# A hybrid decoder step on one core: the first tile's front in another order, one weight place less, two row places more

## What is computed

```
mod = silu(c) @ w_ada + b_ada                       # six vectors per request
h = rmsnorm(x) * (1 + scale1) + shift1
q, k, v, u, gv, gate_a, gate_b = h @ w_in           # 7 x 1024 columns
out_b = stick_breaking_attention(q, k, v)           # 8 heads x 128, no softmax
out_a = u * (w_spatial @ layernorm(gelu(gv)) + b)   # 128 x 128 per channel group
x = x + gate1 * ((gate_a * (out_a @ w_ba) + gate_b * (out_b @ w_bb)) @ w_out)
h = rmsnorm(x) * (1 + scale2) + shift2
for each token and each of 8 heads:                 # retrieval
    scores against 2 x 128 sub-keys -> best 16 of 16 x 16 pairs -> 16 expert numbers
    coef = softmax(best) * gelu(h . down[expert]);  sum += coef * up[expert]
y = rmsnorm(x + gate2 * sum)
```

## Time and profile before

| | us |
|---|---|
| median of three timed runs (lowest, highest) | 2500.59 (2497.98, 2501.23) |
| the profiled execution | 2490.67 |
| its span, first to last instruction | 2488.5 |
| TensorE busy in it | 1888.3 (76%) |
| VectorE busy | 1558.6 (63%) |
| GpSimd busy | 1265.7 (51%) |
| ScalarE busy | 572.2 (23%) |

### The profile page before, as it was taken

How to read it: one execution, slowest core, us unless ns; L and a number is a source line. 1 busy time by engine, 2 the same in 40 slices (tenths; PEclk the granted TensorE clock), 3 DMA queues, 4 the chain that set the end, 5 groups by cost and what they waited for, 6 DMA issues and landing times.

```text
span 2488.5 us, 25049 instructions
## 1 busy us (share of the span) xinstructions
PE 1888.3 (76%) x7944; PEld 1316.6 (53%) x7944; DVE 1558.6 (63%) x3451; ACT 572.2 (23%) x1217; POOL 1265.7 (51%) x1169
## 2 busy tenths in 40 slices
PE   4876879777896767876878699877666577677777
PEld 2666868666775555644655466656454222222222
DVE  1011166789887467754587767675769987767662
ACT  1060121664110112134222310111011122122121
POOL 0000035556664454643556555555557777776763
PEclk7998989898998898987986765888888789999999
DMA  7867779988999797984799889999989999999996
GB/s 271 346 242 241 265 270 376 399 298 341 389 411 359 252 396 284 407 304 168 285 359 378 352 320 371 338 365 365 348 322 343 337 390 395 393 409 408 409 409 269
DMA packets 219219, 845.04 MB, mean 340 GB/s; under 512 B 26576, under 2 KB 35848, under 8 KB 197585
## 3 DMA queue, kind: packets, MB, share of 16 engines
q0 software_dynamic: 165888, 604.05, 63.7%
q1 hardware_dynamic: 36884, 216.87, 23.0%
q10 hardware_dynamic: 16316, 22.52, 2.6%
HBM read 826.29 MB, written 16.80 MB: 339 GB/s over the span
## 4 chain that ended last, share of the span: by engine, by line
PE 39%; DMA 20%; DVE 15%; POOL 8%; issue 8%; ACT 5%; DVEq 5%; SPq 1%; ACTq 1%; POOLq 0%
PE bank L822 12%; PE bank L1138 9%; PE bank L813 8%; DMA gather_ring<-in_expert_down,expert_numbers 8%; DMA gather_ring<-in_expert_up,expert_numbers 4%; DVE expert_sums L1831 4%; POOL gather_ring L778 3%; POOL gather_ring L763 3%; DVE gather_ring L1800 2%; DMA weight_chunks<-in_w_in 2%; DMA v_tokens<-in_expert_up,expert_numbers 1%; POOL weight_chunks L763 1%; DMA key_scores<-key_scores 1%; PE bank L1062 1%; SPq L671 1%
## 5 line engine op out<-in xcount | busy, mean ns | idle before, releaser
L763 POOL DMA_INDIRECT gather_ring<-in_expert_down,expert_numbers x488 | 569.3, 1167 | 797.7 <-DVEq L1763 357.9
L1138 PE MATMUL bank<-gather_ring,coef_diagonals 128*128 128x512 f32 x952 | 566.1, 740 | 327.9 <-ACT coef_diagonals L1416 191.1
L778 POOL DMA_INDIRECT gather_ring<-in_expert_up,expert_numbers x510 | 545.6, 1070 | 346.7 <-PE bank L1138 198.0
L1800 DVE CUSTOM_DVE_ANT_0 gather_ring<-gather_ring,h_tiles 128x1024 f32<-128x1024 f32 x408 | 498.3, 1226 | 234.8 <-DMA gather_ring<-in_expert_down,expert_numbers 213.2
L1138 PEld LDWEIGHTS bank<-gather_ring,coef_diagonals 128*128 128x128 f32 x952 | 204.9, 230 | 617.1 <-issue 370.5
L822 PE MATMUL bank<-hT,weight_chunks 128*128 128x128 f32 (+2 forms) x2304 | 408.3, 339 | 32.6 <-DMA weight_chunks<-in_w_in 19.5
L822 PEld LDWEIGHTS bank<-hT,weight_chunks 128*128 128x128 f32 x2304 | 380.5, 202 | 80.8 <-issue 59.6
L1831 DVE SCALAR_TENSOR_TENSOR expert_sums<-gather_ring,expert_coefs,expert_sums 128x1024 f32<-128x1024 f32 x269 | 345.5, 1285 | 9.4 <-issue 9.4
L813 PE MATMUL bank<-weight_chunks,hT 128*128 128x256 f32 x960 | 219.9, 389 | 20.7 <-DMA weight_chunks<-in_w_in 20.7
L813 PEld LDWEIGHTS bank<-weight_chunks,hT 128*128 128x128 f32 x960 | 185.8, 195 | 54.9 <-DMA weight_chunks<-in_w_in 24.2
L1416 ACT ACTIVATE coef_diagonals<-identity,expert_coefs 128x128 f32<-128x128 f32 x304 | 108.7, 393 | 285.1 <-DVE expert_coefs L1811 126.2
(11 more groups left out here) (242 smaller groups left out, 2109.7 us busy)
## 6 DMA issues: line engine op xcount, KB each, us to landing
weight_chunks<-in_w_in SPq DMA_DIRECT2D x84, 1024.0 KB
weight_chunks<-in_w_ada SPq DMA_DIRECT2D x24, 1024.0 KB
weight_chunks<-in_w_query SPq DMA_DIRECT2D x24, 1024.0 KB
weight_chunks<-in_w_branch_a SPq DMA_DIRECT2D x12, 1024.0 KB
weight_chunks<-in_w_branch_b SPq DMA_DIRECT2D x12, 1024.0 KB
weight_chunks<-in_w_out SPq DMA_DIRECT2D x12, 1024.0 KB
weight_chunks<-in_cache_k SPq DMA_DIRECT2D x16, 512.0 KB
weight_chunks<-in_cache_v SPq DMA_DIRECT2D x16, 512.0 KB
```

The lines of the kernel that those rows point to most:

```text
L763: pool.indirect_dma_start(out=d_row(slot), out_offset=None, in_=down, in_offset=bass.IndirectOffsetOnAxis(ap=expert[:, t, h * TOPK + k:h * ...
L778: pool.indirect_dma_start(out=u_row(slot), out_offset=None, in_=up, in_offset=bass.IndirectOffsetOnAxis(ap=expert[:, t, h * TOPK + k:h * T ...
L1138: mm = nc.tensor.matmul(bank[6 + half], diag[:, n % 8, :], u_row(slot)[:, half * 512:(half + 1) * 512], start=(u == PE_TILE[t][0]), stop=( ...
L1800: nc.vector.tensor_tensor_reduce(out=row, in0=row, in1=x, scale=1.0, scalar=0.0, op0=ALU.mult, op1=ALU.add, accum_out=dots[:, m % 2, k:k + ...
```

## The change

The two row buffers and the weight buffer change sizes: `NW` from 4 to 3, `D_EARLY` from 4 to 5, `U_EARLY` from 5 to 6; together they keep their size. Attention of tile 0 takes four heads at once, with instructions four times as wide, in four steps instead of six. The modulation vectors are stored behind the first three merge chunks, with six stores of the sampled vectors a quarter (one for each vector, repeated over the tokens of a sequence) for the eight of before. The norms of tiles 1 to 4 move into the front of group 0, beside its k chunks. The first head's scores are read where ScalarE leaves them, without the way through memory, and `exponentials(0)` and `weigh(0)` change places in their orders. The numbers `RAISE`, `WEIGH`, `AHEAD` and `LATER` are new names for values that stay as they were.

```diff
-D_EARLY, D_LATE = 4, 8
-U_EARLY, U_LATE = 5, 8
+D_EARLY, D_LATE = 5, 8
+U_EARLY, U_LATE = 6, 8
...
-    size = 2 if g == 0 else 1
+    size = 4 if g == 0 else 1
...
-NW = 4
+NW = 3
...
                 if g == 0:
+                    load_through("merge", g, NW - 1)
                     sp.wait_ge(s_modv, 4 * NMOD)
                     sp.wait_ge(s_mod, 8)
...
                         sp.dma_start(rows[:, :, q], modq[32 * q:32 * q + 1]).then_inc(s_modst, 16)
-                        for i in range(DSEQ):
-                            sp.dma_start(by_token[:, i, :, q], modq[32 * q + 1:32 * q + NG]).then_inc(s_modst, 16)
-                    sp.wait_ge(s_modst, 16 * 4 * (DSEQ + 1))
+                        for m in range(NMOD):
+                            sp.dma_start(by_token[:, :, m, q],
+                                         modq[32 * q + 1:32 * q + NG, m].unsqueeze(1).broadcast_to([NDEC, DSEQ, QUARTER])).then_inc(
+                                             s_modst, 16)
+                    sp.wait_ge(s_modst, 16 * 4 * (NMOD + 1))
...
+                def four_scores(b):
+                    z = bank[4 + b]
+                    nc.tensor.matmul(z[:, :].rearrange("p (j n) -> p j n", j=4), ident[:],
+                                     hidden[:].unsqueeze(1).broadcast_to([P, 4, P]), start=True, stop=False)
+                    for j in range(4):
+                        mm = nc.tensor.matmul(z[:, j * P:(j + 1) * P], kT[:, 0, 4 * b + j, :], q[:, 4 * b + j, 0:P],
+                                              start=False, stop=(j == 3))
+                    mm.then_inc(s_az, 4)
+
+                def four_exponents(b):
+                    pe.wait_ge(s_al, 4 * b + 4)
+                    if b:
+                        pe.wait_ge(s_aw, 4 * b)
+                    log, pos, neg = (att(what, 4 * b, g) for what in ("log", "pos", "neg"))
+                    nc.tensor.matmul(bank[2][:, :], since[:], log, start=True, stop=False)
+                    nc.tensor.matmul(bank[2][:, :], later[:], pos, start=False, stop=False)
+                    nc.tensor.matmul(bank[2][:, :], ident[:], neg, start=False, stop=True).then_inc(s_ac, 4)
...
+                def four_log_parts(b):
+                    log, pos, neg = (att(what, 4 * b, g) for what in ("log", "pos", "neg"))
+                    act.wait_ge(s_az, 4 * b + 4)
+                    for j in range(4):
+                        hd, cols = 4 * b + j, slice(j * P, (j + 1) * P)
+                        z = bank[4 + b][:, cols]
+                        nc.scalar.activation(log[:, cols], z, ACT.Abs, scale=SCALE, bias=bias_b[:, hd:hd + 1])
...
+                    nc.scalar.activation(log, log, ACT.Exp, scale=-1.0)
+                    act.drain()
+                    nc.scalar.activation(log, log, ACT.Ln, bias=1.0).then_inc(s_al, 4)
...
             for n, _ in enumerate(front(0)):
-                if n in (queries + 2, queries + 3):
-                    load_scores(act, n - queries - 2)
+                if n == queries + 3:
+                    load_scores(act, 1)
+                if n == queries + 5:
+                    exponentials(0)
+                    load_scores(act, 2)
             other = chain(front(1), front(2))
-            done = 0
-            exponentials(0)
-            load_scores(act, 2)
...
+            def first_norm(n):
+                x = vv[:, [t for ts in GROUPS for t in ts][n], :]
+                dve.drain()
+                mean_square(x, 0, s_n1v)
+                r = reciprocal_root(s_n1s, n + 1, 0)
+                nc.vector.tensor_scalar(x, x, r, None, ALU.mult).then_inc(s_n1h, 1)
...
                 for c in range(12):
                     if g == 0 and c % 4 == 3:
                         modulation(2 + c // 4)
+                    if g == 0 and 4 <= c < 8:
+                        dve.wait_ge(s_x[1 if c < 6 else 2], 32 * 2)
+                        first_norm(c - 3)
                     yield
...
-                dve.wait_ge(s_scld[c % 2], 16 * (c // 2 + 1))
+                if c:
+                    dve.wait_ge(s_scld[c % 2], 16 * ((c + 1) // 2))
+                    scores = [sc[:, c % 2, a, :] for a in range(2)]
+                else:
+                    dve.wait_ge(s_sev[0], 1)
+                    scores = [sc_out[:, 0, a * NKEY:(a + 1) * NKEY] for a in range(2)]
...
-            weigh(0)
             running = None
...
-                    if c and e == at["weigh"]:
+                    if e == (at["weigh"] if c else 1 - TOPK):
                         weigh(c)
```

84 lines of the change are left out of this document (67 added, 17 removed).

## The result

The changed kernel takes 2467.41 us (median of 13 runs), the kernel before 2491.77 in 13 runs beside it: a ratio of 0.990, interval 0.9882 to 0.9919, so 24 us or 1.0% less. The direction and the range held; the size did not: 73 us were forecast. Some of the distance between 2427 and 2467 is the base, since the three runs known beforehand had a median of 2500.59, nine above that of thirteen.

The account below looks back on a forecast made before the run. Bounds: SyncE's order in the first front, small rings in the middle, rows alone at the end. Terms 7.5 + 11.8 + 8.0 - 1.0 + 47 = 73 us off gave 2427 us on the median; range 2365 to 2490.

Parts of the forecast that it names:

- row places: Middle, 372 to 1960 us: five and six places raise the stretches' rates, 47 us gained, bounds nothing and 213.
- attention in fours and the store: First front: u ends some 10 us earlier, the store takes 25.0 us, fourth merge chunk at 213.2; gain 7.5 us.
- norms of the other tiles: Moved beside group 0's k chunks: 11.8 us gained at the second group, 8.0 at the last.
- three weight places: Each chunk is asked for one use later: 1 us lost in the first front, bounds 0 and 5; nothing later.
- scores in place: End of first front: first gather 9.9 us earlier but off the path, counted at nothing; up to 9.9 without cover.
- What bounds the kernel: First front: SyncE's order makes TensorE's 19.53 us hole; middle: rings with few places for their latency; end: rows alone at 396 GB/s.
- The shape's bound of 1.22 us: First front: upper bound per larger modulation store, if issue grows with the 1 KB pieces; 0.91 us was taken.
- The case that I gave with both against it: First front: 1.22 us per store and no gain in attention together, a loss of some 10 us.
- Places give nothing: Rival, middle: the ring fills more but rows land later by as much; 2474 us, chance 0.25.
- Weights late: Rival, second group: weight chunks land too late behind more rows, places give nothing; 2558 us, chance 0.10.
- Front does not move: Rival: store cancels attention's gain, ScalarE takes up the norms' 11.8 us, places bring little; 2490 to 2503 us, chance 0.07.
- Places give double: Rival, middle: stalls refill faster, half of the 300 us of row waits go; about 2360 us, chance 0.08.

Follow-up runs that it names:

- store_old: Changed kernel with the modulation store in its old place, ahead of all merge chunks, and in its old shape, one small and eight larger stores a quarter; ratio 0.9898.
- pairs: Changed kernel with tile 0's attention in pairs of heads, six steps, as before; ratio 0.9924 to the kernel before.
- front_only: Changed kernel with the old sizes, four weight places and four and five row places, so only the front's new order; ratio 0.9950 to the kernel before.
- norms_back: Changed kernel with the norms of tiles 1 to 4 back at the start of their own groups' fronts; ratio 0.9936 to the kernel before.
- small_rings: Changed kernel with four and five row places again, but still three weight places; ratio 0.9979 to the kernel before.
- scores_dram: Changed kernel with the first head's scores through memory again and the old order of exponentials and softmax; ratio 0.9865 to the kernel before.
- changed_again: The changed kernel once more, unaltered, on the same chip as the runs beside it; ratio 0.9885 to the kernel before.
- store_pool: Changed kernel with the 28 modulation stores issued by GpSimd, SyncE only waiting for them behind the eighth merge chunk; ratio 0.9833 to the kernel before.
- store_once: Changed kernel with sampled vectors stored once per sequence, reads repeating them over the tokens, 8 stores on SyncE instead of 28; ratio 0.9806 to the kernel before.

## Why the prediction came out as it did

Two steps failed. The row places were priced by straight lines through the rates of whole stretches, at 47 us, and gave 23. And the first front, from which nearly 27 us were to come (store and attention, norms of the second group and the last, less 1 for the weights), gave almost nothing, because each of its terms was priced without what comes next in the same queue.

| term of the sum | forecast, us | measured, us | from |
|---|---|---|---|
| attention in fours and the store | -7.5 | 0 (store), -2 to -5 (attention, by traces) | store_old, pairs, front_only |
| norms of the other tiles | -19.8 | -9 | norms_back |
| three weight places | +1 | +7 (trace +9.5) | small_rings, front_only |
| scores in place | 0 | 0 to +9 | scores_dram |
| row places | -47 | -23 | small_rings, changed_again |
| sum | -73 | -18 to -30 | the change: -24 |

Each measured term is a difference of two ratios and uncertain by 7 to 12 us.

*What bounds the kernel.* The reading held: SyncE's order makes the hole (store_pool, store_once), the rings are short for their latency in the middle, and nothing happens behind 1960 us (from the dot of row 400 to the end it takes 519 us before and 521 after).

*Attention and store.* The mechanism was right and the sizes were off. The fourth merge chunk came 17.7 us later than forecast (230.93 for 213.2): 10.1 because the store starts at 188.70 and not at 178.6, 7.3 because it takes 32.3 us and not 25.0. The ten us for two steps counted TensorE's time and not that it would then meet the weights. The shape's bound of 1.22 us a store was the true value, since pieces and not stores set the time. The case that I gave with both against it, a loss of some 10, is the one that came: the first scores are 10.0 us later.

*Norms.* Right where the cover was looked up in the trace of the last group, wrong where I took an idle time as gained without asking what comes last next. I named ScalarE and the products behind it, but not the score stores.

*Weight places.* I took 1 us, with bounds of 0 and 5, from a slice of 346 GB/s that I called close to the limit; the same strip has slices of 390 to 411. The step that failed is that a chunk's delay was priced as transfer time. Its real price in the old order is what SyncE holds behind a place that is not free: the store, and 17.6 us. What makes the 7 to 9.5 us of the new order was not traced chunk by chunk.

*Scores.* "Off the path", I said, and gave it nothing or a gain. There was no gain, so nothing was the right size; a loss of up to 9 us, which I had no case for, is not excluded.

*Row places.* Half of the 47 came. The lines end at the stretch with 16 places, where rows run alone, and so took its whole rate as due to places. Waits for rows fell by 55 to 60 us as they should, but two things took back a part: a row lands 20% later with 22% more places, and VectorE, which is through its rows sooner, waits 27 us longer for scores that ScalarE has not yet asked for. I said that waits overlap; I did not ask what VectorE would wait for next.

*The rivals.* "Places give nothing", 2474, has the nearest time, but not for its reason: the places gave 23 and the front gave little. That rows land later by almost as much is in it, and came. "Weights late" is out: one wait of 5.8 us behind 340 in the changed kernel. "Front does not move" was right about the front: its sign, the fourth merge chunk at 222 or later, came, as did its 1.22 and the norms' time taken up by ScalarE; only "the places bring little" failed. "Places give double" is out (and half of 300 us off the median is 2350, not 2360). As for the rule that 358 GB/s is one core's limit: fifteen of the 40 slices of the changed kernel stand at 392 to 414, so it was no reason for that rival here. The Trainium skill says so itself on another page (Perfetto Trace Analysis, Roofline: more than 100% of that figure is normal for single-core kernels), and the trace agrees with that one.

## What to carry to other kernels

Before a store is moved or reshaped in a full queue, ask whether so much must be written: writing each vector once and not eight times was worth 23 us, moving or regrouping the same pieces nothing that could be measured. When buffer space is shifted from one ring to another, price the ring that loses by what its queue holds behind it, not by its bandwidth. And an engine that waits less for rows arrives earlier at whatever it waits for next: issue the small loads that it needs then earlier, in the same edit.

## What was not expected of the hardware

On SyncE's queue a burst takes as long as its pieces, however they are grouped: 384 pieces of 1 KB took 6.8 to 7.3 us as eight stores before and 6.7 to 7.3 as six with the change. The single stores of a burst differ widely. Of the larger stores, before and then with the change (ns, shortest, median, longest, and first and last start):

```profile
L671 SPq DMA_DIRECT2D mod_sample<-gather_ring x32: 297/862/1557, 169.4 to 199.0; - x32
```

```profile
L693 SPq DMA_DIRECT2D mod_sample<-gather_ring x24: 647/775/1940, 189.5 to 219.1; - x24
```

So 48 pieces can be issued in 0.30 us, and some stores in a burst are held up for a us or more. Full DMA engines are not what holds them: from 197 to 221 us in the changed kernel their share is 0.31, at 50 GB/s. What does was not tested. GpSimd issues the 64 pieces in a median of 0.67 us, but they land a median of 7.5 us after that:

```profile
mod_sample<-gather_ring POOLq DMA_DIRECT2D x24, 64.0 KB, 7.5
```

The Trainium skill (DMA: Bandwidth & Descriptors, Anatomy of one DMA, which is on the path by GpSimd) calls descriptor generation small, with many to be had before the cost shows. The trace agrees for GpSimd, where 6 pieces take 0.59 to 0.73 us and 64 a median of 0.67.

A 128 KB store of key scores that took some 5 us in the kernel before, where it was issued just ahead of the first gather (324.9 to 329.9), took 11.9 us with the change (334.91 to 346.79), with no more than five rows and three weight chunks under way; together they filled the transfers, at 402 GB/s.
